# Entry to the seven-product jobs: order of the sums of x, the root and the first gates, and the engine of each chunk's last y rest

## The chip, the cores and the metric

The kernel runs on one core of a Trainium2 chip. The metric is the device time of one execution in microseconds (us). The kernel before takes 1664.19 us, the median of three runs (1663.05 to 1666.98).

## The reference, cut to what matters

Two transformer blocks in float32 over 512 tokens of width 1024. The change lies in the last part of the first block, the gated feed-forward:

```python
def rmsnorm(x, g):
    xf = x.astype(jnp.float32)
    y = xf * lax.rsqrt(jnp.mean(xf * xf, axis=-1, keepdims=True) + EPS)
    return (y * g.astype(jnp.float32)).astype(x.dtype)

def swiglu(u, w_gate_up, w_down):
    gate, up = jnp.split(u @ w_gate_up, 2, axis=-1)
    return (jax.nn.silu(gate) * up) @ w_down
...
        h = h + memory_cross_attention(...)
        h = h + swiglu(rmsnorm(h, ffn_norm[l]), w_gate_up[l], w_down[l])
    return rmsnorm(h, final_norm)
```

w_gate_up is 1024 x 5632 (D_FF = 2816, 22 tiles of 128), w_down 2816 x 1024.

## The kernel before, in words

**Products in three parts.** Activations lie transposed: features on the partitions, 512 tokens along the free axis. Every float32 product is made of three matmuls on rounded parts: hi = the value rounded to fp32r, lo = the rest; hi x hi, hi x lo and lo x hi are added in a PSUM bank. So every weight and every activation has to be *rounded* (hi) and have its *rest* (lo) taken by some engine before PE can use it. Work is cut into *jobs*, one block of 256 weight columns each. The four PSUM tiles g_bank hold job results, the four banks t_bank everything else, sums of weights and of x among them. Raw weights come by SP's DMAs into two slots w_raw, a job's slot being free when w_split has counted the split of the job two before it.

**Norm.** x_hi and x_lo hold h times the norm's gain, without the division by the root mean square; each product is multiplied by rstd afterwards. ScalarE squares h, VectorE adds the squares (add_squares, L2939), PE sums them over the partitions (squares_sum, task stat3, L1126), ScalarE takes the square root (root, L1872, with an ACT_TABLE_LOAD of its own ahead), and VectorE the reciprocal (L3002).

**Feed-forward.** The 22 tiles are three chunks (FF_CHUNKS = 8, 8, 6). A tile's job (gu) has 128 gate and 128 up columns. The first three tiles (gu0, gu0+1, gu0+2) are plain: 48 matmuls of 512 columns, after which VectorE multiplies the gate by rstd (plain_gate, L3022), ScalarE takes the silu (L2196), VectorE multiplies by up (gated_up, L3029, tile ga; it frees the job's g_bank pair), ScalarE rounds ga to y_hi (y_round), and GpSimd takes y_lo (y_rest, L915). Job gu0+2 uses the g_bank pair of gu0, so PE can start it only when gated_up(0) is done.

The other 19 tiles are made as 2 x 2 blocks with seven products in place of eight (seven_products, L1420). This takes sums of x, computed once, and sums of weights, computed for each tile. The sums of x: ScalarE copies x times gain in full precision to x32a and x32b (eight instructions of 128 x 512), VectorE makes four differences of 128 x 1024 in PSUM (x_sum, L3010; number i into banks 0 and 1 for even i, 2 and 3 for odd i), ScalarE rounds each (x_sum_hi), VectorE takes each rest (x_sum_rest, L3016). Sum i+2 overwrites the banks of sum i, so it waits for rest i. The root's operand lies in one of t_bank's banks 2 and 3. For each tile, ScalarE copies one quarter of the weights (a22_copy), VectorE makes three sums (first_sum, other_sums, L3034 to L3041), ScalarE rounds seven operands, VectorE takes three rests (sum_rest, L3047), GpSimd one difference (difference_of_weights, L893) and four rests (first_rests, last_rest, L899). A tile's fourth block waits for the gate bank of the tile before it (for the first tile: gated_up(2)).

**Chunk end.** A chunk's four down jobs follow its tiles. The first (L1483) goes through y tile by tile and waits for each y_lo (ff_lo); its weights are rounded by ScalarE into e_hi, and GpSimd takes the rest e_lo (subtract_hi, L879). The second's weights are split wholly by GpSimd (plain_split, L885 and L879) into w_hi and w_lo. In the last chunk the third and fourth are rounded by ScalarE (L2279) and their rests taken by GpSimd (L954).

**What orders the work.** Each engine's instructions stand in the order in which its block is written; semaphores alone join them. In the order before, the entry on ScalarE is: root, copies to x32, x_sum_hi(0) and (1), silu(0), x_sum_hi(2) and (3), y_round(0), silu(1), y_round(1). On VectorE: reciprocal, x_sum(0), x_sum(1), rest(0), x_sum(2), gate(0), rest(1), x_sum(3), rest(2), gated_up(0), rest(3), gate(1), gated_up(1). On GpSimd: the split of gu0+2's weights, y_rest(0), y_rest(1), then the first tile. At a chunk's end GpSimd has e_lo, the last y_rest, then the second down job's split:

```python
                pool.wait_ge(slot_hi, down_hi_count(c))
                pool.nop().then_inc(pool_chain, 1)
                subtract_hi(down, e_lo[:], e_hi[:], n)
                y_rest(c, FF_F0[c] + n - 1)
                pool.wait_ge(block_done, BLOCK0 + 6 * s + 4)
                plain_split(down + 1, w_lo[:, 0], w_hi[:, 0])
```

Of the kernel before, what the change touches and what calls it, by code (L numbers as in the profile page):

```python
# [20 lines left out]
ALU = mybir.AluOpType  # L21
ACT = mybir.ActivationFunctionType
AX = mybir.AxisListType
F32 = mybir.dt.float32
# [58 lines left out]
FF_F0 = [0, 8, 16]  # L83
# [148 lines left out]
def program(nc, A, out):  # L232
    with ExitStack() as ctx:
# [544 lines left out]
        def _(pool):  # L778
# [122 lines left out]
            def first_rests(c, j, s):  # L901

                slot_rest(c, s, 0, w_part_raw(j, 0, 0)).then_inc(slot_lo, 1)
                slot_rest(c, s, 1, w_part_raw(j, 1, 0)).then_inc(slot_lo, 1)
                slot_rest(c, s, 4, s3_raw[:]).then_inc(slot_lo, 1)
# [5 lines left out]
            def y_rest(c, tile):  # L911

                pool.wait_ge(ff_hi, tile + 1)
                k = tile - FF_F0[c]
                nc.gpsimd.tensor_tensor(y_lo[:, k, :], ga[:, tile % 2, :], y_hi[:, k, :].bitcast(F32), ALU.subtract).then_inc(ff_lo, 1)  # L915
# [4 lines left out]
            for c, n in enumerate(FF_CHUNKS):  # L920
                tiles = ff_tiles(c)
                down = JOBS[f"down{c}"]
                j, tile, s = tiles[0]
                if c == 0:
                    y_rest(c, 0)
                    y_rest(c, 1)
                difference_of_weights(j, s)
                first_rests(c, j, s)
                for i, (j, tile, s) in enumerate(tiles):
                    more = i + 1 < len(tiles)  # L930
                    if more:
                        difference_of_weights(j + 1, s + 1)
                    last_rest(c, j, s)
                    if tile > FF_F0[c]:
                        y_rest(c, tile - 1)
                    if more:
                        first_rests(c, j + 1, s + 1)
                pool.wait_ge(slot_hi, down_hi_count(c))
                pool.nop().then_inc(pool_chain, 1)
                subtract_hi(down, e_lo[:], e_hi[:], n)  # L940
                y_rest(c, FF_F0[c] + n - 1)
                pool.wait_ge(block_done, BLOCK0 + 6 * s + 4)
                plain_split(down + 1, w_lo[:, 0], w_hi[:, 0])
                if c < 2:
                    pool.wait_ge(w_used, down)
                    plain_split(down + 2, w_lo[:, 1], w_hi[:, 1])
                    pool.wait_ge(w_used, down + 1)
                    plain_split(down + 3, e_lo[:], e_hi[:])
# [903 lines left out]
        def _(act):  # L1852
            def copy(o, i, scale=1.0):
                return nc.scalar.activation(o, i, ACT.Copy, scale=scale)  # L1854
# [15 lines left out]
            def root(i, e=0):  # L1870
                b = ready(i)
                ins = nc.scalar.activation(rstd[:], b, ACT.Sqrt, bias=eps[:, e:e + 1], scale=1.0 / D)  # L1872
                link(ins)
                act.nop().then_inc(t_free[BANK[i]], 1)
                act.nop().then_inc(std_ready, 1)
# [297 lines left out]
            for i in range(4):  # L2173
# [4 lines left out]
                    copy(x_hi[:, k, :], hT[:, k, :], col["ffn_norm"](k)).then_inc(nhi_ready, 1)  # L2178
                for k in (2 * i, 2 * i + 1):
                    square(2, k)  # L2180
            root(TASKS["stat3"])

            act.wait_ge(w_used, JOBS["gu0"])
            for k in range(DT):
                ins = copy(x32[k // HK][:, k % HK, :], hT[:, k, :], col["ffn_norm"](k))
            ins.then_inc(slot_hi, 1)

            def x_sum_hi(i):

                act.wait_ge(sum_ready, 16 + max(i + 1, 2))  # L2190
                copy(xt_hi[i][:], sum_banks(i % 2)).then_inc(slot_hi, 1)

            def silu(tile, bank_):

# [20 lines left out]
                act.wait_ge(slot_lo_v, LO_V0 + 3 * s)  # L2215
                copy(sum_bank(2), w_part_raw(j, 1, 1)).then_inc(a22_ready, 1)

            x_sum_hi(0)
            x_sum_hi(1)
            silu(0, 0)  # L2220
            x_sum_hi(2)
            x_sum_hi(3)
            y_round(0, 0)
            silu(1, 2)
            y_round(0, 1)
            for c, n in enumerate(FF_CHUNKS):
# [392 lines left out]
        def _(dve):  # L2619
# [378 lines left out]
                done(v.tensor_tensor(y_lo[:, i, :], b, y_hi[:, i, :].bitcast(F32), ALU.subtract), o_lo, t_free[BANK[r]])  # L2998

            residual_and_lo(JOBS["wo1"], 2, col["ffn_norm"], x_hi, x_lo)  # L3000
            dve.wait_ge(std_ready, 2)
            link(v.reciprocal(rstd[:], rstd[:]))  # L3002
            for b in range(4):
                dve.wait_ge(t_free[b], FF_BEFORE[b])

            def x_sum(i, out, in0, in1):

# [16 lines left out]
            def gated_up(j, tile, up):  # L3024

                dve.wait_ge(sg_ready, tile + 1)
                if tile >= 2:
                    dve.wait_ge(ff_lo, tile - 1)
                done(v.tensor_tensor(ga[:, tile % 2, :], sg[:, tile % 2, :], up, ALU.mult), ga_ready, g_free[j % 2])  # L3029

            def first_sum(j, s):

# [21 lines left out]
            def add_down(c, i):  # L3054
# [10 lines left out]
                if c == 2:  # L3065
                    add_squares(3, i)

            dve.wait_ge(slot_hi, 1)
            x_sum(0, sum_banks(0), x32_part(0, 1), x32_part(0, 0))
            x_sum(1, sum_banks(1), x32_part(1, 1), sum_banks(0))  # L3070
            x_sum_rest(0)
            x_sum(2, sum_banks(0), x32_part(1, 1), x32_part(0, 1))
            plain_gate(0)
            x_sum_rest(1)
            x_sum(3, sum_banks(1), x32_part(1, 0), sum_banks(1))
            x_sum_rest(2)
            gated_up(JOBS["gu0"], 0, g_bank[:, 1, :])
            x_sum_rest(3)
            plain_gate(1)
            gated_up(JOBS["gu0"] + 1, 1, g_bank[:, 3, :])  # L3080
            for c, n in enumerate(FF_CHUNKS):
# [14 lines left out]
                for i, (j, tile, s) in enumerate(tiles):  # L3096
# [21 lines left out]
                    up_halves = g_bank[:, up, :].rearrange("p (a b) -> p a b", b=HT)  # L3118
                    link(v.tensor_tensor(up_halves, up_halves, m_sum[:, V, :].unsqueeze(1).to_broadcast([P, 2, HT]), ALU.add))
                    gated_up(j, tile, g_bank[:, up, :])  # L3120
                add_down(c, 0)
                add_down(c, 1)
            add_down(2, 2)
# [412 lines left out]
```

## Time and profile before

| | before |
|---|---|
| median of 3 runs | 1664.19 us (1663.05 to 1666.98) |
| profiled execution, own time | 1664.38 us |
| its span | 1662.7 us |
| mean granted TensorE clock | 0.997 of full |
| busy: PE, DVE, ACT, POOL | 98%, 63%, 40%, 63% |
| this stage, from the first plain job to the last down job | about 512.5 to 869.6 us |

The profile is of one execution. Its own time is the span plus what lies around it. Engines are PE (TensorE), DVE (VectorE), ACT (ScalarE), POOL (GpSimd) and SP (the queue that issues DMAs). In a timeline row the brackets give the engine's idle time just before the row and what ended it. Matmuls overlap in the pipeline, so a matmul's duration is longer than the distance between two starts. L1420 is line 1420 of the kernel; a helper's line stands for all its callers.

### The profile page before, as it was taken

To read this page: it belongs to the slowest core of one execution; us is meant where nothing else is said; L and a number is where in the kernel's file an instruction comes from. 1 tells how busy PE (TensorE), PEld (TensorE's weight loads), DVE (VectorE), ACT (ScalarE), POOL (GpSimd) and SP (SyncE) were. 2 spreads that over 40 slices of the span, in tenths; PEclk is the share of its full clock that TensorE was granted. 3 is DMA by queue.
4 is the path that set the end of the run, shared out by engine and by line. 5 is a ranking of instruction groups with operands and counts; after the bars stand their busy time and mean duration, and the time that the engine had idled before them with its cause. 6 is when DMAs were issued, how large, how long until landed. Compare 5 with 4: busy or idle time off the path is not lost.

```text
span 1662.7 us, 23770 instructions
## 1 busy us (share of the span) xinstructions
PE 1630.6 (98%) x8755; PEld 1384.0 (83%) x8755; DVE 1041.3 (63%) x1631; ACT 664.2 (40%) x1166; POOL 1040.3 (63%) x791
## 2 busy tenths in 40 slices
PE   7999999999998999999999999999999999999998
PEld 5898897888977998998978888887878778877887
DVE  5323948772446645745747898999646686556624
ACT  5431238330424523523525545674312245555301
POOL 7675764566656675775766788785467644334664
PEclk9999999999999999999999999999999999999999
DMA  6333333233243233433334333222243222111231
GB/s 210 122 108 112 118 102 121 83 101 102 83 145 101 67 112 90 111 105 93 98 105 111 101 102 95 79 81 77 76 152 97 89 76 76 53 51 52 76 114 64
DMA packets 188347, 162.59 MB, mean 98 GB/s; under 512 B 7636, under 2 KB 184400, under 8 KB 187728
## 3 DMA queue, kind: packets, MB, share of 16 engines
q1 hardware_dynamic: 188040, 161.10, 30.5%
q8 instruction: 67, 1.10, 0.3%
q14 instruction: 40, 0.33, 0.1%
q10 hardware_dynamic: 200, 0.06, 0.0%
HBM read 155.87 MB, written 4.23 MB: 96 GB/s over the span
## 4 chain that ended last, share of the span: by engine, by line
PE 90%; DVE 5%; ACT 2%; POOL 1%; issue 1%; DMA 1%; DVEq 0%; SPq 0%; ACTq 0%; POOLq 0%
PE g_bank L1046 53%; PE g_bank L1420 9%; PE g_bank L1080 6%; PE g_bank L1070 5%; PE t_bank L1759 2%; PE t_bank L1420 2%; PE g_bank L1483 1%; PE g_bank L1629 1%; PE t_bank L1771 1%; PE t_bank L1371 1%; PE t_bank L1403 1%; PE t_bank L1748 1%; PE t_bank L1547 1%; PE t_bank L1568 1%; PE g_bank L1220 1%
## 5 line engine op out<-in xcount | busy, mean ns | idle before, releaser
L803 POOL TENSOR_SCALAR w_hi<-w_raw 128x2048 fp32r<-128x2048 f32 x67 | 132.5, 1978 | 387.3 <-PE g_bank L1046 160.8
L820 POOL TENSOR_TENSOR w_lo<-w_raw,w_hi 128x512 fp32r<-128x512 f32 x264 | 367.0, 1421 | 5.5
L1046 PE MATMUL g_bank<-x_hi,w_hi 128*128 128x512 f32 x912 | 364.5, 400 | 0.4 <-DVEq L2633 0.4
L1046 PE MATMUL g_bank<-x_hi,w_lo 128*128 128x512 f32 x912 | 355.5, 390 | 0.0
L1046 PE MATMUL g_bank<-x_lo,w_hi 128*128 128x512 f32 x912 | 355.2, 390 | 0.0
L1046 PEld LDWEIGHTS g_bank<-x_hi,w_hi 128*128 128x128 f32 x912 | 171.3, 188 | 38.8 <-issue 4.8
L1046 PEld LDWEIGHTS g_bank<-x_hi,w_lo 128*128 128x128 f32 x912 | 171.2, 188 | 36.1
L1046 PEld LDWEIGHTS g_bank<-x_lo,w_hi 128*128 128x128 f32 x912 | 171.5, 188 | 35.1 <-issue 1.4
L3165 DVE SCALAR_TENSOR_TENSOR t_bank<-hc,cols,t_bank 128x512 f32<-128x512 f32 x280 | 187.0, 749 | 4.5 <-DVE hc L3149 2.7
L954 POOL TENSOR_TENSOR w_lo<-w_raw,w_hi 128x512 fp32r<-128x512 f32 x100 | 127.4, 1309 | 62.7 <-ACT w_hi L2279 62.7
L1046 PE MATMUL g_bank<-y_hi,w_hi 128*128 128x512 f32 x288 | 113.6, 394 | 2.4 <-POOL w_lo L879 2.4
L1046 PE MATMUL g_bank<-y_hi,w_lo 128*128 128x512 f32 x288 | 112.2, 390 | 0.0
L1046 PE MATMUL g_bank<-y_lo,w_hi 128*128 128x512 f32 x288 | 112.1, 389 | 0.0
L899 POOL TENSOR_TENSOR w_lo<-w_raw,w_hi 128x512 fp32r<-128x512 f32 x57 | 73.0, 1296 | 34.0 <-ACT w_hi L1854 34.0
L972 POOL TENSOR_TENSOR pacc<-pacc,prod 128x512 f32<-128x512 f32 x54 | 68.1, 1293 | 0.0
L1046 PEld LDWEIGHTS g_bank<-y_hi,w_hi 128*128 128x128 f32 x288 | 54.1, 188 | 14.9 <-POOL w_lo L879 2.8
L1420 PE MATMUL g_bank<-x_hi,w_lo 128*128 128x256 f32 x228 | 64.5, 283 | 0.0
L1420 PE MATMUL g_bank<-xt_hi,w_hi 128*128 128x256 f32 x228 | 64.5, 283 | 0.0
L1420 PE MATMUL g_bank<-xt_lo,w_hi 128*128 128x256 f32 x228 | 64.5, 283 | 0.0
L1420 PE MATMUL g_bank<-xt_hi,w_lo 128*128 128x256 f32 x228 | 64.5, 283 | 0.0
L1420 PE MATMUL g_bank<-x_lo,w_hi 128*128 128x256 f32 x228 | 64.5, 283 | 0.0
L1420 PE MATMUL g_bank<-x_hi,w_hi 128*128 128x256 f32 x228 | 64.5, 283 | 0.0
(564 smaller groups left out, 3985.3 us busy)
## 6 DMA issues: line engine op xcount, KB each, us to landing
w_raw<-w_gate_up SPq DMA_DIRECT2D x44, 512.0 KB, 4.7
w_raw<-a_w_in SPq DMA_DIRECT2D x44, 512.0 KB, 4.5
w_raw<-b_w_in SPq DMA_DIRECT2D x38, 512.0 KB, 4.4
w_raw<-w_in SPq DMA_DIRECT2D x28, 512.0 KB, 4.5
w_raw<-w_kv SPq DMA_DIRECT2D x16, 512.0 KB, 3.9
w_raw<-w_out_mix SPq DMA_DIRECT2D x16, 512.0 KB, 6.4
w_raw<-w_down SPq DMA_DIRECT2D x16, 512.0 KB, 4.1
w_raw<-a_w_out SPq DMA_DIRECT2D x16, 512.0 KB, 4.4
```

The costliest lines, as they stand in the source:

```text
L803: nc.gpsimd.tensor_scalar(w_hi[:, par], w_raw[:, par], 1.0, 0.0, ALU.mult, ALU.add).then_inc(pool_chain, 1)
L820: last = nc.gpsimd.tensor_tensor(w_lo[:, par, s], w_raw[:, par, s], w_hi[:, par, s].bitcast(F32), ALU.subtract)
L899: return nc.gpsimd.tensor_tensor(lo, src, hi.bitcast(F32), ALU.subtract)
L954: last = nc.gpsimd.tensor_tensor(lo[:, s], w_raw[:, j % 2, s], hi[:, s].bitcast(F32), ALU.subtract)
L972: nc.gpsimd.tensor_tensor(acc_k[:], acc_k[:], p[:], ALU.add).then_inc(tap_chain, 1)
L1046: last = nc.tensor.matmul(g_bank[:, 2 * pair + f if banks is None else banks[f], 0:n], ww[:, k0 + k, ws], xk, start=(k == 0 and q == 0), s ...
L1070: last = nc.tensor.matmul(g_bank[:, 2 * par + f, :], ww[:, par, k, ws], xx[:, k0 + k, :], start=(k == 0 and q == 0), stop=(k == kt - 1 and ...
L1080: last = nc.tensor.matmul(g_bank[:, 2 * par + m // 2, m % 2 * WC:m % 2 * WC + n], xx[:, k, m * P:(m + 1) * P], ww[:, k, 0:n], start=(k == ...
L1220: last = nc.tensor.matmul(g_bank[:, 2 * (j % 2) + f, :], ww[:, k, ws], xx[:, k, :], start=(k == 0 and q == 0), stop=(k == KT - 1 and q == 2))
L1420: last = nc.tensor.matmul(out, ww[:, k, :], xx[:, k, :], start=(k == 0 and q == 0), stop=(k == HK - 1 and q == 2))
L1759: last = nc.tensor.matmul(b[:, c:c + W_OF[qb]], qB[:, 4 * hg + i, qb * P:(qb + 1) * P], kB[:, 0:W_OF[qb]], start=True, stop=True)
L3165: ins = v.scalar_tensor_tensor(tail if k == TAPS - 1 else a(k), h(k), wk, a(k), ALU.mult, ALU.add)
```

## The change

Three edits. (1) ScalarE makes the copies to x32 and rounds the first sum of x ahead of the root, and VectorE makes that sum and its rest ahead of the reciprocal; only the banks that a sum writes are waited for (0 and 1, later 2 and 3). (2) The first gate product, silu and gated_up(0) stand ahead of sums 2 and 3, and y_round(0) ahead of rounding sum 2; GpSimd's y_rest(1) goes behind the first tile's first rests. (3) The last y rest of each chunk is taken by VectorE (last_y_rest) and no longer by GpSimd. PE's and SP's programs stay as they are.

```diff
--- before.py
+++ after.py
@@ -923,9 +923,10 @@
                 j, tile, s = tiles[0]
                 if c == 0:
                     y_rest(c, 0)
-                    y_rest(c, 1)
                 difference_of_weights(j, s)
                 first_rests(c, j, s)
+                if c == 0:
+                    y_rest(c, 1)
                 for i, (j, tile, s) in enumerate(tiles):
                     more = i + 1 < len(tiles)
                     if more:
@@ -938,7 +939,6 @@
                 pool.wait_ge(slot_hi, down_hi_count(c))
                 pool.nop().then_inc(pool_chain, 1)
                 subtract_hi(down, e_lo[:], e_hi[:], n)
-                y_rest(c, FF_F0[c] + n - 1)
                 pool.wait_ge(block_done, BLOCK0 + 6 * s + 4)
                 plain_split(down + 1, w_lo[:, 0], w_hi[:, 0])
                 if c < 2:
@@ -2178,17 +2178,18 @@
                     copy(x_hi[:, k, :], hT[:, k, :], col["ffn_norm"](k)).then_inc(nhi_ready, 1)
                 for k in (2 * i, 2 * i + 1):
                     square(2, k)
-            root(TASKS["stat3"])
+
+            def x_sum_hi(i):
+
+                act.wait_ge(sum_ready, 16 + i + 1)
+                copy(xt_hi[i][:], sum_banks(i % 2)).then_inc(slot_hi, 1)
 
             act.wait_ge(w_used, JOBS["gu0"])
             for k in range(DT):
                 ins = copy(x32[k // HK][:, k % HK, :], hT[:, k, :], col["ffn_norm"](k))
             ins.then_inc(slot_hi, 1)
-
-            def x_sum_hi(i):
-
-                act.wait_ge(sum_ready, 16 + max(i + 1, 2))
-                copy(xt_hi[i][:], sum_banks(i % 2)).then_inc(slot_hi, 1)
+            x_sum_hi(0)
+            root(TASKS["stat3"])
 
             def silu(tile, bank_):
 
@@ -2215,12 +2216,11 @@
                 act.wait_ge(slot_lo_v, LO_V0 + 3 * s)
                 copy(sum_bank(2), w_part_raw(j, 1, 1)).then_inc(a22_ready, 1)
 
-            x_sum_hi(0)
+            silu(0, 0)
             x_sum_hi(1)
-            silu(0, 0)
+            y_round(0, 0)
             x_sum_hi(2)
             x_sum_hi(3)
-            y_round(0, 0)
             silu(1, 2)
             y_round(0, 1)
             for c, n in enumerate(FF_CHUNKS):
@@ -2998,10 +2998,6 @@
                 done(v.tensor_tensor(y_lo[:, i, :], b, y_hi[:, i, :].bitcast(F32), ALU.subtract), o_lo, t_free[BANK[r]])
 
             residual_and_lo(JOBS["wo1"], 2, col["ffn_norm"], x_hi, x_lo)
-            dve.wait_ge(std_ready, 2)
-            link(v.reciprocal(rstd[:], rstd[:]))
-            for b in range(4):
-                dve.wait_ge(t_free[b], FF_BEFORE[b])
 
             def x_sum(i, out, in0, in1):
 
@@ -3027,6 +3023,13 @@
                 if tile >= 2:
                     dve.wait_ge(ff_lo, tile - 1)
                 done(v.tensor_tensor(ga[:, tile % 2, :], sg[:, tile % 2, :], up, ALU.mult), ga_ready, g_free[j % 2])
+
+            def last_y_rest(c, tile):
+
+                k = tile - FF_F0[c]
+                dve.wait_ge(ff_hi, tile + 1)
+                dve.wait_ge(ff_lo, tile)
+                v.tensor_tensor(y_lo[:, k, :], ga[:, tile % 2, :], y_hi[:, k, :].bitcast(F32), ALU.subtract).then_inc(ff_lo, 1)
 
             def first_sum(j, s):
 
@@ -3065,16 +3068,22 @@
                 if c == 2:
                     add_squares(3, i)
 
+            for b in range(2):
+                dve.wait_ge(t_free[b], FF_BEFORE[b])
             dve.wait_ge(slot_hi, 1)
             x_sum(0, sum_banks(0), x32_part(0, 1), x32_part(0, 0))
+            x_sum_rest(0)
+            dve.wait_ge(std_ready, 2)
+            link(v.reciprocal(rstd[:], rstd[:]))
+            plain_gate(0)
+            for b in range(2, 4):
+                dve.wait_ge(t_free[b], FF_BEFORE[b])
             x_sum(1, sum_banks(1), x32_part(1, 1), sum_banks(0))
-            x_sum_rest(0)
+            gated_up(JOBS["gu0"], 0, g_bank[:, 1, :])
             x_sum(2, sum_banks(0), x32_part(1, 1), x32_part(0, 1))
-            plain_gate(0)
             x_sum_rest(1)
             x_sum(3, sum_banks(1), x32_part(1, 0), sum_banks(1))
             x_sum_rest(2)
-            gated_up(JOBS["gu0"], 0, g_bank[:, 1, :])
             x_sum_rest(3)
             plain_gate(1)
             gated_up(JOBS["gu0"] + 1, 1, g_bank[:, 3, :])
@@ -3118,6 +3127,7 @@
                     up_halves = g_bank[:, up, :].rearrange("p (a b) -> p a b", b=HT)
                     link(v.tensor_tensor(up_halves, up_halves, m_sum[:, V, :].unsqueeze(1).to_broadcast([P, 2, HT]), ALU.add))
                     gated_up(j, tile, g_bank[:, up, :])
+                last_y_rest(c, tile)
                 add_down(c, 0)
                 add_down(c, 1)
             add_down(2, 2)
```

VectorE at the entry, from the end of the sums of squares to the second gated product; before (xt_lo_134 to xt_lo_137 are the rests of the sums of x 0 to 3):

```order
L3002 RECIPROCAL rstd<-rstd 128x512
L3010 TENSOR_TENSOR t_bank<-x32a 128x1024
L3010 TENSOR_TENSOR t_bank<-x32b,t_bank 128x1024
L3016 TENSOR_TENSOR xt_lo_134<-t_bank,xt_hi_130 128x1024
L3010 TENSOR_TENSOR t_bank<-x32b,x32a 128x1024
L3022 TENSOR_TENSOR g_bank<-g_bank,rstd 128x512
L3016 TENSOR_TENSOR xt_lo_135<-t_bank,xt_hi_131 128x1024
L3010 TENSOR_TENSOR t_bank<-x32b,t_bank 128x1024
L3016 TENSOR_TENSOR xt_lo_136<-t_bank,xt_hi_132 128x1024
L3029 TENSOR_TENSOR ga<-sg,g_bank 128x512
```

The same place in the changed kernel:

```order
L3006 TENSOR_TENSOR t_bank<-x32a 128x1024
L3012 TENSOR_TENSOR xt_lo_134<-t_bank,xt_hi_130 128x1024
L3077 RECIPROCAL rstd<-rstd 128x512
L3018 TENSOR_TENSOR g_bank<-g_bank,rstd 128x512
L3006 TENSOR_TENSOR t_bank<-x32b,t_bank 128x1024
L3025 TENSOR_TENSOR ga<-sg,g_bank 128x512
L3006 TENSOR_TENSOR t_bank<-x32b,x32a 128x1024
L3012 TENSOR_TENSOR xt_lo_135<-t_bank,xt_hi_131 128x1024
L3006 TENSOR_TENSOR t_bank<-x32b,t_bank 128x1024
L3012 TENSOR_TENSOR xt_lo_136<-t_bank,xt_hi_132 128x1024
L3012 TENSOR_TENSOR xt_lo_137<-t_bank,xt_hi_133 128x1024
L3018 TENSOR_TENSOR g_bank<-g_bank,rstd 128x512
```

Sum 0 and its rest went ahead of the reciprocal. Between reciprocal and first ga there were eight instructions, now there are two.

ScalarE at the entry, as one piece of the difference:

```order
 L1854 ACTIVATE x_hi<-hT,cols 128x512 x2
 L2111 ACTIVATE nring<-hT 128x512 x2
-L1872 ACT_TABLE_LOAD
-L1872 ACTIVATE rstd<-t_bank,eps 128x512
 L1854 ACTIVATE x32a<-hT,cols 128x512 x4
 L1854 ACTIVATE x32b<-hT,cols 128x512 x4
 L1854 ACTIVATE xt_hi_130<-t_bank 128x1024
+L1872 ACT_TABLE_LOAD
+L1872 ACTIVATE rstd<-t_bank,eps 128x512
+L2197 ACT_TABLE_LOAD
+L2197 ACTIVATE sg<-g_bank 128x512
 L1854 ACTIVATE xt_hi_131<-t_bank 128x1024
```

The root with its table load went behind the eight copies and the rounding of sum 0.

GpSimd at the end of chunk 2 (the same piece stands at the ends of chunks 0 and 1, with x4 for e_lo):

```order
 L915 TENSOR_TENSOR y_lo<-ga,y_hi 128x512
 L879 TENSOR_TENSOR e_lo<-w_raw,e_hi 128x512 x3
-L915 TENSOR_TENSOR y_lo<-ga,y_hi 128x512
 L885 TENSOR_SCALAR w_hi<-w_raw 128x2048
 L879 TENSOR_TENSOR w_lo<-w_raw,w_hi 128x512 x4
```

The split of the second down job's weights now stands right behind e_lo.

## Rows read from the trace of the kernel before

**Rows 1.** the page, busy time of the engines
```profile
PE 1630.6 (98%) x8755; PEld 1384.0 (83%) x8755; DVE 1041.3 (63%) x1631; ACT 664.2 (40%) x1166; POOL 1040.3 (63%) x791
```

**Rows 2.** timeline of PE at the entry: start us, us, engine, line, operation, tiles
```profile
534.89 0.39 PE L1046 MATMUL g_bank<-x_hi,w_lo 128*128 128x512 f32 x1
541.86 0.77 PE L1046 MATMUL g_bank<-x_hi,e_hi 128*128 128x512 f32 x1 [6.58 <-DVEq L2633]
...
555.25 0.28 PE L1420 MATMUL g_bank<-x_hi,w_hi 128*128 128x256 f32 x1
```

**Rows 3.** granted clock and busy times, 542 to 549 us: window; length; busy us (instructions)
```profile
542.00:549.00 7.00, 7.00 (x21) 5.55 (x22) 4.40 (x6) 3.65 (x8) 4.50 (x4) 0.65 0.01 2
```

**Rows 4.** chain of waits, entry: start us, us, what
```profile
512.61 10.88 PE g_bank L1070 x48
```

**Rows 5.** waits of PE, 560 to 870 us: us in total, times, longest us
```profile
PE g_bank L1046 <- POOL w_lo L879: 2.4, 1, 2.4
```

**Rows 6.** timeline of ACT at the entry
```profile
515.89 1.28 ACT L1872 ACT_TABLE_LOAD   x1
524.39 0.69 ACT L1872 ACTIVATE rstd<-t_bank,eps 128x512 f32<-128x512 f32 x1 [7.21 <-PE t_bank L1126]
525.28 2.56 ACT L1854 ACTIVATE x32a<-hT,cols 128x512 f32<-128x512 f32 x4 [0.20 <-ACT rstd L1872]
...
532.95 1.94 ACT L1854 ACTIVATE xt_hi<-t_bank 128x1024 fp32r<-128x1024 f32 x2 [2.66 <-DVE t_bank L3010]
```

**Rows 7.** timeline of DVE at the entry
```profile
516.88 3.48 DVE L2939 TENSOR_TENSOR sq_sum<-sq_sum,nring 128x512 f32<-128x512 f32 x2
525.31 3.35 DVE L3002 RECIPROCAL rstd<-rstd 128x512 f32<-128x512 f32 x1 [4.95 <-ACTq L1875]
530.42 1.23 DVE L3010 TENSOR_TENSOR t_bank<-x32a 128x1024 f32<-128x1024 f32 x1 [1.76 <-ACT x32b L1854]
...
540.88 0.68 DVE L3029 TENSOR_TENSOR ga<-sg,g_bank 128x512 f32<-128x512 f32 x1
...
544.29 0.69 DVE L3029 TENSOR_TENSOR ga<-sg,g_bank 128x512 f32<-128x512 f32 x1 [0.66 <-ACT sg L2196]
...
550.54 0.69 DVE L3047 TENSOR_TENSOR w_lo<-t_bank,w_hi 128x512 fp32r<-128x512 f32 x1 [0.21 <-ACT w_hi L1854]
```

**Rows 8.** all instructions of line 2939: durations in ns, min/median/max
```profile
L2939 DVE TENSOR_TENSOR sq_sum<-sq_sum,nring x21: 678/1666/1778, 352.0 to 873.2; 128x512 f32<-128x512 f32 x21
```

**Rows 9.** timeline of ACT, a table load elsewhere
```profile
874.73 1.28 ACT L2289 ACT_TABLE_LOAD   x1
876.03 0.20 ACT L2289 ACTIVATE ltok<-eps 128x1 f32<-128x1 f32 x1
```

**Rows 10.** timeline of POOL at the entry
```profile
521.48 1.91 POOL L885 TENSOR_SCALAR e_hi<-w_raw 128x2048 fp32r<-128x2048 f32 x1
523.48 5.04 POOL L879 TENSOR_TENSOR e_lo<-w_raw,e_hi 128x512 fp32r<-128x512 f32 x4
```

**Rows 11.** timeline of PE after chunk 2's first down job
```profile
844.64 0.50 PE L1046 MATMUL g_bank<-y_hi,w_hi 128*128 128x512 f32 x1 [2.38 <-POOL w_lo L879]
```

**Rows 12.** timeline of POOL around the end of chunk 2
```profile
828.22 3.80 POOL L879 TENSOR_TENSOR e_lo<-w_raw,e_hi 128x512 fp32r<-128x512 f32 x3 [0.17 <-ACT e_hi L1854]
836.33 1.28 POOL L915 TENSOR_TENSOR y_lo<-ga,y_hi 128x512 fp32r<-128x512 f32 x1 [4.32 <-ACT y_hi L1854]
...
839.59 5.00 POOL L879 TENSOR_TENSOR w_lo<-w_raw,w_hi 128x512 fp32r<-128x512 f32 x4
844.54 5.47 POOL L954 TENSOR_TENSOR w_lo<-w_raw,w_hi 128x512 fp32r<-128x512 f32 x4
```

**Rows 13.** w_raw, 824 to 842 us: DMA issues, time to landing
```profile
L604 SPq DMA_DIRECT2D w_raw<-w_down x4: 367/428/489, 826.6 to 832.5; - x4
...
DMA to landing us min/median/max: 3.0/3.5/3.8
```

**Rows 14.** timeline of ACT after chunk 2's first down job
```profile
842.29 1.91 ACT L2279 ACTIVATE w_hi<-w_raw 128x2048 fp32r<-128x2048 f32 x1 [6.04 <-PE g_bank L1483]
```

## The prediction

> **What bounds the kernel now.** The page comes first: TensorE (PE) is busy for 98% of the span, the other compute engines for 40 to 63% [rows 1]. So time can come only from what PE waits for and from the clock at which it works; a faster VectorE (DVE), ScalarE (ACT) or GpSimd (POOL) is worth nothing by itself. I looked for PE's gaps where the change is. The timeline shows one at the entry: the last matmul of job gu0+1 begins at 534.89, the first of gu0+2 at 541.86, after 6.58 us of idling that ended with a semaphore from VectorE [rows 2]. The matmul behind the gap takes 0.77 instead of 0.39, and from 542 to 549 the granted clock is 0.65 of full, so PE sat partly at the lower level, 1.2 GHz, after that idle stretch [rows 3]. A job of 48 matmuls at full clock takes 10.88 [rows 4]; gu0+2 takes 13.39, from 541.86 to the first matmul of the seven-product tile at 555.25 [rows 2]. The whole rest of the stage, 560 to 870, holds one more wait, 2.4 us for a split by GpSimd [rows 5].
>
> **The entry, before.** ScalarE has loaded the square root's table by 517.2 and then idles 7.21 until the root at 524.39; only behind it come the eight copies of x [rows 6]. VectorE idles 4.95, takes the reciprocal at 525.31 (3.35), waits for the copies and starts the first sum at 530.42. The first gate product ends at 541.56 (540.88 + 0.68), and PE starts 0.30 later [rows 7, 2].
>
> **The entry, after, step by step.** The copies need 5.14 (525.28 until the sum that they release at 530.42). They can start where the table load stands now, 515.89, so they release VectorE at 521.03; its sums of squares end at 520.36 (516.88 + 3.48) [rows 6, 7].
> x_sum(0) takes 1.23 with GpSimd idle. It reads two tiles in SBUF, and now GpSimd is splitting weights beside it. That is not in the trace of before for this operation; the nearest row is the sum of squares, which also reads two SBUF tiles: 0.68 at least, 1.78 at most [rows 8]. I take the difference, 1.1, since that row was taken beside the same work: 2.33, to 523.36. Bounds: 0, and 1.9 for waiting out GpSimd's whole rounding of 1.91 [rows 10].
> The Trainium skill, page "SBUF — State Buffer", section Who interferes with whom, says that such a DVE instruction and a GpSimd one that reads SBUF exclude each other for a whole instruction; by it the upper bound would be the value. The entry sum would end near 524.6 and PE would be served about 0.8 later than worked out here.
> Then x_sum_hi(0) 1.0 (two took 1.94), the table load 1.28, no longer hidden, and the root 0.69 [rows 6]: 526.35. PE has the root's operand ready at 524.36, so the root moves 2 us later; this is the price of putting the sum ahead. Reciprocal 0.23 behind the root and 3.35 long: 529.95. Gate product 0.69, x_sum(1) 1.24 with the silu (0.66) beside it, ga 0.68, release 0.30 [rows 7]: PE may start at **532.9**. It is free at 534.89 + 0.23 = 535.12, so 2.2 us are spare, 1.4 at the upper bound, 3.3 at the lower. GpSimd's split of the weights of gu0+2 ends at 528.5 (523.48 + 5.04) [rows 10], with 1.9 of delay at 530.4: also in time. The gap goes whole: 541.86 - 535.12 = **6.74**.
> Without the gap nothing asks the clock to fall: gu0+2 takes 10.88 and not 13.39: **2.51**. Its end is then 546.0.
> A page states more for the table load. The trace has 1.28 for it, and elsewhere an activation starts 0.02 after such a load ended [rows 9]. "ScalarE: Activation LUTs", section What ACT_TABLE_LOAD costs, in the Trainium skill, adds a drain of some 1.38 to each switch; by it the gate would still come in time, and the next step would be late (rival 1).
>
> **What is late next.** The three sums and four rests left over now stand between the first and the second gate. From the end of ga(0), 532.6: five operations of 1.24, gate product, silu: ga(1) starts at 540.15 (in the old order 3.4 after ga(0), now 7.5). From the start of ga(1) to the end of the last rest of the first tile's sums it was 550.54 + 0.69 - 544.29 = 6.94 [rows 7]: 547.1. Gate(2), silu and ga(2) add 0.69 + 0.66 + 0.69, and 0.30: 549.45. The fourth block of the first tile waits for that; it is due at 546.0 plus three blocks of 12 half-width matmuls, 1.36 each, 550.1. Spare: 0.6 us; at the upper bound of the first sum a wait of 0.2, at the lower 1.7 spare. Should x_sum(2) also meet a GpSimd operation (1.1), 0.5 to 1.3 are lost. I take 0. GpSimd's own first rests, 1.28 each [rows 12], come before the second y rest now, and are due at 546.0 and 547.4; started near 543 they end at 544.3 and 545.6. The moved y rest and the next difference have till 556.1.
>
> **The chunk ends.** In chunk 2 PE ends the first down job and waits 2.38 for w_lo of the second [rows 11]. GpSimd had finished e_lo at 832.02, idled 4.32 for the last y_hi, made y_lo (1.28), and only then split the second job's weights, 836.33 + 1.28 to 844.59, 6.98 long [rows 12]. With the y rest on VectorE the split starts at 832.02 and ends at 839.0, for a PE that is free at 842.10. The load is no new wait: issued from 826.6 in two parts, at most 3.8 to land, so there by about 831 [rows 13]. The rest on VectorE reads two SBUF tiles, 0.68 to 1.78 by rows 8, from about 836.35; its engine is idle there, and PE needs y_lo for the sixth step near 840.7. It may hold GpSimd's split up by 0.7, into 3 us of spare. Gain: 844.64 - 842.10 = **2.54**. Next late is the third job: ScalarE rounds from 842.29 for 1.91 [rows 14], GpSimd takes 5.47 [rows 12], so 849.7; PE comes at 842.10 + 8.16 (36 matmuls) = 850.3. Spare 0.6. In chunks 0 and 1 PE has no wait at this place [rows 5], so the same edit is worth nothing there.
>
> **The sum.** 6.74 + 2.51 + 2.54 = 11.8 off the profiled execution's 1664.38: 1652.6. Against the median of the runs, 1664.19, it is **1652.4**. The profiled execution stands 0.2 above that median.
>
> **Rivals.** 0.2% of the time, 3.3 us, is about what a measurement here can tell from no change.
> 1. *The fourth block waits.* For: 0.6 of spare is less than one contended operation. Against: no such wait at 557, and the steps are priced from rows. With 1.2 lost, 1653.6. An idle of some 1.4 behind the new table load, which rows 9 speak against, would end in the same place: 0.8 lost, 1653.2, and I give it 0.02 of this rival's chance. That is the drain that the Trainium skill's page "ScalarE: Activation LUTs" names in the section cited above.
> 2. *The chunk end does not pay*: GpSimd is held up, or the third job's weights take the same 2.5. For: 0.6 spare there too. 1654.9.
> 3. *GpSimd holds the first sum until its whole split is done*, 528.5. The sum then ends at 529.75, 6.4 later: PE starts gu0+2 at 539.3, with 4.2 of the gap left and perhaps the slow clock (0 to 2.5). The gain at the entry is 2.5 to 5.0; about 1658.5. Against: in rows 8 no operation lost more than 1.1.
> 4. *The change does not do what it says*, since the gate still comes at 541.6 for a cause that I don't see; with the chunk end, 1661.7, no change that can be told.
> 5. *Slower.* Engines enter the 19 seven-product tiles with less in hand, and GpSimd, last in line for each tile, holds PE up in all of them instead of once. Its price is the lag per tile: over 11.8 / 19 = 0.62 us in each the change loses, and at 0.9 it would give 1664.2 - 11.8 + 17.1 = 1669.5. For: GpSimd starts the first tile 4 us later relative to PE than before. Against: six operations of 1.28 are 7.7 us in a tile of at least 7 x 1.36 = 9.5, so a lag shrinks by about 2 us in each.
>
> **How the numbers follow.** Forecast 0.73; rival 1 0.12, rival 2 0.06, rival 3 0.04, rival 4 0.03, rival 5 0.02. Cases 1 to 3 and the forecast are faster by more than 3.3: 0.95; rival 4 is the same: 0.03; rival 5 slower: 0.02. The range reaches below by 1.9, since both medians may be off by about the 1.1 that the lowest run of before lies under its own, and above to rivals 1 and 2 together, 1652.4 + 1.2 + 2.5 = 1656.1. It is 1650.5 to 1656.1.
>
> **What would show it.** Right: no PE wait between 534 and 556, clock 1.00 in the stretch of gu0+2, L1872 at about 525.7, reciprocal near 526.6, first ga end near 532.6, no wait for the split in front of chunk 2's second down job. Wrong in part: a PE wait ahead of the fourth block of the first tile, or one in front of the third down job. Wrong as a whole: x_sum(0) longer than 3.1 us, or short waits in many L1420 blocks.

## The result and the profile after

The changed kernel takes 1652.34 us, the median of four runs (1651.63 to 1652.55); the kernel before took 1663.89 beside it (four runs, 1663.05 to 1666.98). The ratio is 0.9926, with a 95% interval of 0.9914 to 0.9938. The prediction was 1652.4, with a range of 1650.5 to 1656.1.

The profiled execution of the changed kernel took 1652.55 us, its span is 1650.8, 11.9 less than before. The page, its busy times and the order of the engines in them, as [rows 1]:

```profile
PE 1627.0 (99%) x8755; PEld 1381.9 (84%) x8755; DVE 1046.3 (63%) x1634; ACT 664.6 (40%) x1166; POOL 1039.3 (63%) x788
```

PE at the three places of [rows 2], the last matmul of gu0+1, the first of gu0+2, the first of the seven-product tiles:

```profile
534.86 0.39 PE L1046 MATMUL g_bank<-x_hi,w_lo 128*128 128x512 f32 x1
535.08 0.39 PE L1046 MATMUL g_bank<-x_hi,e_hi 128*128 128x512 f32 x1
...
545.96 0.28 PE L1420 MATMUL g_bank<-x_hi,w_hi 128*128 128x256 f32 x1
```

No idle time stands in a bracket, the first matmul of gu0+2 has its 0.39, and the job takes 545.96 - 535.08 = 10.88. The clock in the windows that held the gap and the slow matmuls (window, length, then busy us and instructions of PE, PEld, DVE, ACT, POOL, then the granted clock, DMA share and GB/s), as [rows 3]:

```profile
535.00:542.00 7.00, 7.00 (x33) 5.79 (x32) 5.05 (x6) 3.46 (x6) 0.68 (x2) 1.00 0.00 0
542.00:549.00 7.00, 7.00 (x45) 6.30 (x44) 5.16 (x9) 4.97 (x11) 6.27 (x6) 1.00 0.00 0
```

The waits of PE from 505 to 860, asked as in [rows 5], are none. The chain of waits through the entry, start and length in us, is now PE alone, where VectorE and ScalarE stood in it before:

```profile
512.58 10.88 PE g_bank L1070 x48
523.46 0.86 PE t_bank L1126 x2
524.32 21.81 PE g_bank L1046 x96
546.13 2.87 PE g_bank L1420 x24
```

VectorE at the entry, as [rows 7] (the sum of x is at line 3006, its rest at 3012, the reciprocal at 3077, the gate at 3018, ga at 3025, the first tile's rests at 3050):

```profile
516.86 3.48 DVE L2939 TENSOR_TENSOR sq_sum<-sq_sum,nring 128x512 f32<-128x512 f32 x2
520.88 1.69 DVE L3006 TENSOR_TENSOR t_bank<-x32a 128x1024 f32<-128x1024 f32 x1 [0.54 <-ACT x32b L1854]
523.74 1.22 DVE L3012 TENSOR_TENSOR xt_lo<-t_bank,xt_hi 128x1024 fp32r<-128x1024 f32 x1 [1.16 <-ACT xt_hi L1854]
525.79 3.35 DVE L3077 RECIPROCAL rstd<-rstd 128x512 f32<-128x512 f32 x1 [0.83 <-ACTq L1875]
529.18 0.70 DVE L3018 TENSOR_TENSOR g_bank<-g_bank,rstd 128x512 f32<-128x512 f32 x1
529.79 1.22 DVE L3006 TENSOR_TENSOR t_bank<-x32b,t_bank 128x1024 f32<-128x1024 f32 x1
531.04 0.69 DVE L3025 TENSOR_TENSOR ga<-sg,g_bank 128x512 f32<-128x512 f32 x1
...
539.39 0.69 DVE L3025 TENSOR_TENSOR ga<-sg,g_bank 128x512 f32<-128x512 f32 x1 [0.67 <-ACT sg L2197]
...
545.64 0.69 DVE L3050 TENSOR_TENSOR w_lo<-t_bank,w_hi 128x512 fp32r<-128x512 f32 x1 [0.20 <-ACT w_hi L1854]
...
547.60 0.69 DVE L3025 TENSOR_TENSOR ga<-sg,g_bank 128x512 f32<-128x512 f32 x1 [0.66 <-ACT sg L2197]
```

ScalarE, as [rows 6]:

```profile
515.74 2.56 ACT L1854 ACTIVATE x32a<-hT,cols 128x512 f32<-128x512 f32 x4
...
522.61 1.03 ACT L1854 ACTIVATE xt_hi<-t_bank 128x1024 fp32r<-128x1024 f32 x1 [1.86 <-DVE t_bank L3006]
523.65 1.28 ACT L1872 ACT_TABLE_LOAD   x1
524.95 0.69 ACT L1872 ACTIVATE rstd<-t_bank,eps 128x512 f32<-128x512 f32 x1
525.82 1.28 ACT L2197 ACT_TABLE_LOAD   x1 [0.18 <-ACT rstd L1872]
```

GpSimd, as [rows 10]:

```profile
521.46 2.88 POOL L885 TENSOR_SCALAR e_hi<-w_raw 128x2048 fp32r<-128x2048 f32 x1
524.42 5.02 POOL L879 TENSOR_TENSOR e_lo<-w_raw,e_hi 128x512 fp32r<-128x512 f32 x4
532.73 1.62 POOL L915 TENSOR_TENSOR y_lo<-ga,y_hi 128x512 fp32r<-128x512 f32 x1 [3.28 <-ACT y_hi L1854]
```

The end of chunk 2, GpSimd and then VectorE, as [rows 12]:

```profile
818.86 3.80 POOL L879 TENSOR_TENSOR e_lo<-w_raw,e_hi 128x512 fp32r<-128x512 f32 x3 [0.18 <-ACT e_hi L1854]
822.63 1.91 POOL L885 TENSOR_SCALAR w_hi<-w_raw 128x2048 fp32r<-128x2048 f32 x1
824.63 5.51 POOL L879 TENSOR_TENSOR w_lo<-w_raw,w_hi 128x512 fp32r<-128x512 f32 x4
834.94 5.49 POOL L954 TENSOR_TENSOR w_lo<-w_raw,w_hi 128x512 fp32r<-128x512 f32 x4 [4.81 <-ACT w_hi L2279]
```

```profile
826.93 0.80 DVE L3032 TENSOR_TENSOR y_lo<-ga,y_hi 128x512 fp32r<-128x512 f32 x1 [0.76 <-ACT y_hi L1854]
```

**Where the time came from.** The profile was cut by starts on PE. All columns are distances in us: from the sum of squares (L1126) to the first matmul of gu0+2; from there to the first seven-product matmul; from there to chunk 0's first down job; in chunk 2 from the first down job to the second; from that to the first memory job. The last is the whole stage from the sum of squares to the memory job, with the parts between that are not shown (they sum to 228.20 to 228.27 in every row). The first rows are the two kernels; the others are the experiments below.

| kernel | to gu0+2 | gu0+2 | tiles of chunk 0 | down job, chunk 2 | to memory job | stage |
|---|---|---|---|---|---|---|
| before | 18.53 | 13.39 | 50.39 | 10.73 | 24.79 | 346.10 |
| after | 11.78 | 10.88 | 50.40 | 8.18 | 24.67 | 334.11 |
| e1_entry_only | 11.78 | 10.88 | 50.40 | 10.72 | 24.82 | 336.86 |
| e2_rest_only | 18.52 | 12.88 | 50.39 | 8.19 | 24.64 | 342.82 |
| e3_rest_last_chunk | 11.79 | 10.88 | 50.39 | 8.18 | 24.66 | 334.10 |
| e4_gates_late | 13.67 | 11.00 | 50.39 | 8.19 | 24.68 | 336.13 |
| e5_root_first | 11.79 | 11.54 | 51.32 | 8.18 | 24.64 | 335.67 |
| e6_delay1 | 11.79 | 10.88 | 50.39 | 8.19 | 24.66 | 334.11 |
| e6_delay3 | 11.79 | 11.27 | 51.34 | 8.18 | 24.69 | 335.47 |
| e6_delay6 | 15.50 | 12.58 | 50.40 | 8.18 | 24.69 | 339.55 |
| e7_second_y_rest_first | 11.79 | 10.88 | 50.39 | 8.18 | 24.65 | 334.09 |
| e8_y_rest_first_and_delay3 | 11.79 | 12.67 | 50.46 | 8.19 | 24.64 | 335.95 |

The stage lost 11.99: 6.75 of the gap, 2.51 of the slow clock behind it, 2.55 in chunk 2, 0.12 in front of the memory job, and the rest in the parts not shown. The whole time of one execution moves by about 1 us from one to the next for a cause outside the stage (PE's first wait, for a DMA of parameters, lasted from 9.1 to 10.6 us in these profiles), so the stage tells tenths apart where the medians don't.

### The profile page after: what moved, and what is told of

It is laid out like the page before. It is cut to its first block, busy times and chain, and to the rows that moved or that the text cites. A ratio compares the mean times of both kernels' runs of the same rounds, so it can differ in the third digit from the quotient of the medians.

```text
span 1650.8 us, 23774 instructions
## 1 busy us (share of the span) xinstructions
PE 1627.0 (99%) x8755; PEld 1381.9 (84%) x8755; DVE 1046.3 (63%) x1634; ACT 664.6 (40%) x1166; POOL 1039.3 (63%) x788
## 4 chain that ended last, share of the span: by engine, by line
PE 93%; DVE 4%; ACT 1%; DMA 1%; issue 1%; POOL 0%; DVEq 0%; SPq 0%; ACTq 0%
PE g_bank L1046 54%; PE g_bank L1420 10%; PE g_bank L1080 6%; PE g_bank L1070 5%; PE g_bank L1483 2%; PE t_bank L1420 2%; PE t_bank L1759 2%; PE g_bank L1629 1%; PE t_bank L1771 1%; PE t_bank L1371 1%; PE t_bank L1403 1%; PE t_bank L1748 1%; PE t_bank L1547 1%; PE t_bank L1568 1%; PE g_bank L1611 1%; PE t_bank L1304 1%
## 5 line engine op out<-in xcount | busy, mean ns | idle before, releaser
L1046 PEld LDWEIGHTS g_bank<-y_hi,w_hi 128*128 128x128 f32 x288 | 54.1, 188 | 11.9 <-issue 0.7
```

Source lines behind the costliest of these rows:

```text
L1046: last = nc.tensor.matmul(g_bank[:, 2 * pair + f if banks is None else banks[f], 0:n], ww[:, k0 + k, ws], xk, start=(k == 0 and q == 0), s ...
```

## The experiments

The theory: the gain is PE's two waits and the clock lost behind the longer one, and nothing else; the entry is worth 9.3, the chunk-end edit 2.5, in chunk 2 alone. Rivals: the relief of GpSimd at all chunk ends carries much of it; the early sum, or the early gate, alone carries the entry; VectorE's chain is the bound at the entry, so that each of its delays costs.

**The entry alone: e1_entry_only.**

```diff
 subtract_hi(down, e_lo[:], e_hi[:], n)
+y_rest(c, FF_F0[c] + n - 1)
...
-last_y_rest(c, tile)
```

> The changed kernel with each chunk's last y rest back on GpSimd. Theory: the entry carries 9.3 us (6.7 of gap, 2.5 of slow clock) and the chunk ends 2.5, so this takes about 1654.9 and PE waits 2.4 us for w_lo in front of chunk 2's second down job, and nowhere else between 505 and 860. Rival (GpSimd, relieved at three chunk ends, carries a good part of the gain): well above 1656.

Measured: 1655.51 us, ratio to the kernel before 0.9951 (0.9938 to 0.9965). Its only wait of PE between 505 and 862 (us in total, times, longest):

```profile
PE g_bank L1047 <- POOL w_lo L879: 2.4, 1, 2.4
```

GpSimd in the same kernel has the old order, with 4.32 of idling for the last y_hi ahead of the y rest:

```profile
818.76 3.80 POOL L879 TENSOR_TENSOR e_lo<-w_raw,e_hi 128x512 fp32r<-128x512 f32 x3 [0.17 <-ACT e_hi L1855]
826.88 1.28 POOL L915 TENSOR_TENSOR y_lo<-ga,y_hi 128x512 fp32r<-128x512 f32 x1 [4.32 <-ACT y_hi L1855]
828.13 1.92 POOL L885 TENSOR_SCALAR w_hi<-w_raw 128x2048 fp32r<-128x2048 f32 x1
830.13 4.99 POOL L879 TENSOR_TENSOR w_lo<-w_raw,w_hi 128x512 fp32r<-128x512 f32 x4
```

The stage is 2.75 longer than in the changed kernel, 2.54 of it at this wait. The rival asked for well over 1656, and falls: outside the wait the relief of GpSimd is worth 0.2.

**The chunk ends alone: e2_rest_only.**

```diff
 subtract_hi(down, e_lo[:], e_hi[:], n)
-y_rest(c, FF_F0[c] + n - 1)
...
+last_y_rest(c, tile)
 add_down(c, 0)
```

> The kernel before with only the last y rests moved to VectorE. Theory: 2.5 us under the kernel before, about 1661.5; the 6.6 us wait at the entry and the slow clock behind it stay as they were. Rival: 5 us or more are gained, since GpSimd is free 4 us earlier at three places.

Measured: 1661.39 us, ratio 0.9982 (0.9973 to 0.9991). The down job in chunk 2 went from 10.73 to 8.19, as with the whole change. The wait at the entry is there with its 6.6:

```profile
PE g_bank L1045 <- DVEq L2632: 6.6, 1, 6.6
```

The stage is 3.28 shorter than before, 0.7 more than the wait. Of that, 0.51 is gu0+2 at 12.88 in place of 13.39: behind the same 6.58 of idling PE worked for a shorter time at the low clock (the last section has the rows). So the price of the slow clock differed by half a microsecond between these two executions, for a cause that is not in the edit.

**Chunk 2 only: e3_rest_last_chunk.**

```diff
 subtract_hi(down, e_lo[:], e_hi[:], n)
+if c < 2:
+    y_rest(c, FF_F0[c] + n - 1)
...
-last_y_rest(c, tile)
+if c == 2:
+    last_y_rest(c, tile)
```

> The changed kernel with the last y rest on VectorE in chunk 2 only, on GpSimd in chunks 0 and 1. Theory: the same time as the changed kernel, 1652.3, no wait of PE between 505 and 860. Rival (GpSimd's earlier release at the first two chunk ends is worth something too): slower than the changed kernel by up to 2.5 us a chunk.

Measured: 1651.65 us, ratio 0.9921 (0.9908 to 0.9935), and a stage of 334.10 against 334.11. The moved rests of chunks 0 and 1 are worth nothing, though GpSimd is free 4 us earlier there too: PE never waited for it at these places. It was close: in this kernel the old order ends chunk 0's split at 607.22 (602.20 + 5.02) and PE starts the second down job at 607.41; in chunk 1 it is 731.39 for 731.60. What sets chunk 2 apart is its six tiles in place of eight. The old order ends the split 10.7 behind the start of the first down job in both (607.22 - 596.51 here, 844.59 - 833.91 in chunk 2 of the kernel before), but with 36 matmuls and not 48 that job takes 8.19 there and not 10.90.

**The early sum without the early gate: e4_gates_late.**

```diff
 # ScalarE
-silu(0, 0)
 x_sum_hi(1)
-y_round(0, 0)
+silu(0, 0)
 x_sum_hi(2)
 x_sum_hi(3)
+y_round(0, 0)
 # VectorE
-plain_gate(0)
 x_sum(1, ...)
-gated_up(JOBS["gu0"], 0, ...)
 x_sum(2, ...)
+plain_gate(0)
 x_sum_rest(1)
 x_sum(3, ...)
 x_sum_rest(2)
+gated_up(JOBS["gu0"], 0, ...)
 x_sum_rest(3)
```

> The changed kernel with the first gate, silu and ga back behind sums 1, 2 and 3; sum 0 stays ahead of the root. Theory: behind the reciprocal (ending at 529.1) stand six operations of 1.2 and the gate's 0.6 before ga: ga ends at 536.8, PE is served at 537.1 and wants to start at 535.1, so a wait of 2.0; about 1654.3 if TensorE's clock stays full, up to 1656.8 if it falls as it did behind the 6.6 us wait. Rival (the sums ahead of the root are what closes the gap, the place of the gate does not count): 1652.3, no wait.

Measured: 1653.66 us, ratio 0.9939 (0.9926 to 0.9953), with one wait:

```profile
PE g_bank L1046 <- DVEq L2633: 1.7, 1, 1.7
```

gu0+2 starts 1.9 later than in the changed kernel, for a forecast of 2.0, so the rival (the place of the gate does not count) falls. The job takes 11.00: the granted clock stayed at 1.00 behind 1.73 of idling. So the early sum alone gives back some 4.9 of the 6.75 of the gap and nearly all of the slow clock; the early gate is worth the last 2.0.

**The early gate without the early sum: e5_root_first.** Some waits go back to those of the kernel before and are not shown here: x_sum_hi(0) waits for two sums again, and VectorE for all four banks at once.

```diff
 # ScalarE
+root(TASKS["stat3"])
 act.wait_ge(w_used, JOBS["gu0"])
 for k in range(DT):
     ins = copy(x32[...], ...)
 ins.then_inc(slot_hi, 1)
-x_sum_hi(0)
-root(TASKS["stat3"])
 silu(0, 0)
+x_sum_hi(0)
 x_sum_hi(1)
 # VectorE
+dve.wait_ge(std_ready, 2)
+link(v.reciprocal(rstd[:], rstd[:]))
+plain_gate(0)
 x_sum(0, ...)
-x_sum_rest(0)
-dve.wait_ge(std_ready, 2)
-link(v.reciprocal(rstd[:], rstd[:]))
-plain_gate(0)
 x_sum(1, ...)
 gated_up(JOBS["gu0"], 0, ...)
+x_sum_rest(0)
 x_sum(2, ...)
```

> The changed kernel with the root ahead of the copies and of sum 0 again, and the reciprocal and the first gate ahead of all sums. Theory: ga(0) ends near 533.6 and is in time for PE at 535.1, so the gap stays closed; but all eight sums and rests stand behind the reciprocal, ga(1) starts near 542.6 instead of 539.4, and PE waits about 1.5 us at the fourth block of the first seven-product tile: 1653.8. Rival (the early sum is needed to close the gap): a wait of several us in front of job gu0+2, 1656 or more.

Measured: 1653.87 us, ratio 0.994 (0.9926 to 0.9953). The gap in front of gu0+2 is closed, by the gate alone; the rival falls. Two short waits come in its place:

```profile
PE g_bank L1420 <- DVEq L2633: 0.6, 1, 0.6
PE g_bank L1420 <- POOL w_lo L899: 0.5, 1, 0.5
```

(A listed wait is shorter than the time lost between starts, since the matmul ahead counts as busy to its modelled end and the first one behind is longer: 0.39 and not 0.28 at the fourth block.) The sum of the losses was right (1.56 by the stage, 1.5 expected), their place only in part. 0.9 fell on the fourth block, as named; 0.66 on the first block, where PE waited for GpSimd's rest of the first slot, which I had counted as in time. All of VectorE's eight sums and rests stand between the first gate and ga(1) here (in the changed kernel two of them stand ahead of the reciprocal), and ga(1) sets when ScalarE rounds that slot, since y_round(1) is ahead of it in ScalarE's queue:

```profile
528.83 0.70 DVE L3018 TENSOR_TENSOR g_bank<-g_bank,rstd 128x512 f32<-128x512 f32 x1
530.56 1.23 DVE L3006 TENSOR_TENSOR t_bank<-x32a 128x1024 f32<-128x1024 f32 x1 [1.03 <-ACT x32b L1854]
...
542.82 0.69 DVE L3025 TENSOR_TENSOR ga<-sg,g_bank 128x512 f32<-128x512 f32 x1 [0.67 <-ACT sg L2196]
```

So each of the two moves closes most or all of the gap alone. Together they are 1.6 to 2.0 us better than either, and each is limited by another wait.

**How much is spare: e6_delay1, e6_delay3, e6_delay6.** Rest 0 of the sums of x is done again, to the same place, one, three or six times.

```diff
 x_sum_rest(0)
+dve.wait_ge(slot_lo_v, 17)
+for _ in range(1):          # 3 in e6_delay3, 6 in e6_delay6
+    link(v.tensor_tensor(xt_lo[0][:], sum_banks(0), xt_hi[0][:].bitcast(F32), ALU.subtract))
 dve.wait_ge(std_ready, 2)
```

> The changed kernel with rest 0 of the sums of x done once more on VectorE ahead of its wait for the root: 1.3 us more, of which 0.8 fall into its idle time there, so gate and sums come 0.5 later. Theory: spare are 3.0 us at the start of gu0+2 and 1.7 at the fourth block, so nothing is lost: 1652.3, no wait. Rival (VectorE's chain is the bound of the entry): 0.5 us slower.

One execution, 1653.09 us; no wait of PE, and a stage of 334.11, the same as without the delay. VectorE's chain is not the bound.

> Rest 0 three times more. Theory: the chain is 3.2 us later: 0.2 lost at the start of gu0+2 and 1.3 at the fourth block of the first tile, together the delay less the spare 1.7: 1653.8. Rival: 3.2 lost, 1655.5.

One execution, 1653.56 us. The stage is 1.36 longer. The reciprocal starts at 528.35, against 525.79 in the changed kernel; all of PE's events up to there lie 0.45 earlier in this profile (gu0 begins at 511.97 and not at 512.42), so the chain is 3.0 later, and 3.0 less the spare 1.7 is 1.3. But the loss again has two places:

```profile
PE g_bank L1420 <- DVEq L2633: 0.6, 1, 0.6
PE g_bank L1420 <- POOL w_lo L899: 0.2, 1, 0.2
```

0.39 at the first block and 0.94 until the fourth. At the start of gu0+2 nothing was lost, where 0.2 was expected.

> Rest 0 six times more. Theory: the chain is 7.3 us later: PE waits 4.2 in front of gu0+2. If TensorE's clock stays full behind it, another 1.4 is lost at the fourth block, 1657.9; if it falls as behind the 6.6 us wait of the kernel before, 4.2 and up to 2.5 are lost and the fourth block does not wait, 1659.0.

One execution, 1658.09 us, the stage 5.44 longer: 3.7 in front of gu0+2 and 1.7 in gu0+2 itself, which took 12.58; no wait at the fourth block. The delay was 6.8 and not 7.3 (six repeats took 7.52), and 6.8 less the spare of 3.05 is 3.7. So the clock did fall, and for a while only: it was at the lower level from 539.60 to 543.01, and half of these 3.41 us is the 1.7. PE behind the wait:

```profile
538.68 0.47 PE L1046 MATMUL g_bank<-x_hi,e_hi 128*128 128x512 f32 x1 [3.55 <-DVEq L2633]
538.98 0.39 PE L1046 MATMUL g_bank<-x_lo,e_hi 128*128 128x512 f32 x1
...
539.45 0.50 PE L1046 MATMUL g_bank<-x_hi,e_hi 128*128 128x512 f32 x1
539.75 0.63 PE L1046 MATMUL g_bank<-x_lo,e_hi 128*128 128x512 f32 x1
...
542.31 0.63 PE L1046 MATMUL g_bank<-x_lo,e_hi 128*128 128x512 f32 x1
...
543.10 0.40 PE L1046 MATMUL g_bank<-x_hi,e_hi 128*128 128x512 f32 x1
543.33 0.39 PE L1046 MATMUL g_bank<-x_lo,e_hi 128*128 128x512 f32 x1
```

**The second y rest: e7_second_y_rest_first and, with the delay, e8_y_rest_first_and_delay3.**

```diff
 y_rest(c, 0)
+y_rest(c, 1)
 difference_of_weights(j, s)
 first_rests(c, j, s)
-if c == 0:
-    y_rest(c, 1)
```

> The changed kernel with GpSimd's second y rest back in front of the first tile's difference and rests. Theory: GpSimd's rest for the first block then ends near 544.7 (y rest 1.3 and difference 1.3 behind the second y_hi at 540.8) for a PE that comes at 546.0: no wait, the stage from the sum of squares to the first memory job as long as in the changed kernel, 334.1. Rival (this third part carries some of the gain): PE waits at the first block.

One execution, 1652.56 us, stage 334.09: this part of the change is worth nothing by itself. What the old place does is push GpSimd's first rest from 541.92 to 542.99, by 1.46, since PE's events lie 0.39 earlier in this profile; the spare time there is 2.6.

> The same edit together with rest 0 done three times more on VectorE. With the delay alone PE lost 0.4 at the first block (GpSimd) and 1.0 at the fourth (VectorE), 1.4 in all. Theory: y rest and difference push GpSimd's first rest to about 547.9, so PE loses 2.0 at the first block and nothing at the fourth: stage 336.1. Rival (GpSimd's order does not matter): 335.5, as with the delay alone.

One execution, 1653.7 us, stage 335.95: 0.5 more than the same delay with the new order of GpSimd. 1.79 was lost at the first block, where 2.0 was expected, and 0.06 until the down job. PE's one wait is at the first block (timeline; the bracket has the idle time and what ended it):

```profile
547.01 0.36 PE L1419 MATMUL g_bank<-x_hi,w_hi 128*128 128x256 f32 x1 [1.59 <-POOL w_lo L899]
```

So the order of GpSimd matters only when the chain ahead of it is late; in the changed kernel it isn't.

## Why the prediction was right, step by step

- **What bounds.** PE's waits were the right thing to count. The gap went whole: 18.53 - 11.78 = 6.75 against 6.74; the clock 2.51 against 2.51; chunk 2's down job 2.55 against 2.54. e1, e2 and e3 show that these parts stand apart and add up: 9.3 at the entry, 2.5 in chunk 2, nothing in chunks 0 and 1. That the sum is right to a tenth is in part luck: the term for the clock was read off one execution, and from that of e2_rest_only, with the same gap, it would have been 2.00.
- **The first sum beside GpSimd.** Priced 2.33, it took 1.69 (bounds 1.23 to 3.1). GpSimd paid too: its rounding of 128 x 2048, 1.91 in [rows 10], took 2.88. In e5, where the same sum runs at 530.56 with GpSimd idle, it takes 1.23, and in that kernel GpSimd's rounding has its 1.91 back. The Trainium skill, page "SBUF — State Buffer", section Who interferes with whom, has an exclusive lock for such a pair. This trace fits it: the sum was issued at 520.88 with GpSimd's last quarter of a split running until 521.46, waited for that, and GpSimd's next instruction, begun at 521.46, took 0.97 more, about the 1.1 that the sum still ran. What I had wrong is which GpSimd instruction the sum would meet: the end of a quarter, not the whole rounding. The prediction's two figures for that case also don't agree: behind the whole rounding the sum would end at 521.48 + 1.91 + 1.23 = 524.6, which is 1.3 later than the 523.36 of the forecast and not 0.8; 0.8 goes with a hold of 1.9 from 521.03.
- **The root behind the sum.** Forecast for its activation 525.66, happened 524.95; for the reciprocal 526.6, 525.79; for the release of PE 532.9, about 532.0 (531.04 + 0.69 + 0.30). The spare time was 3.05 and not 2.2, inside the bounds of 1.4 to 3.3. The price of putting the sum ahead was overstated in the words: 2 us is how long the forecast root ends behind its operand; against the old place, 524.39, the root was to start 1.3 later and started 0.56 later.
- **The table load.** The root started 0.02 after its load had ended (523.65 + 1.28, then 524.95), so the load cost 1.28 and no drain behind it. The page "ScalarE: Activation LUTs", section What ACT_TABLE_LOAD costs, in the Trainium skill, adds 1.38 to that; here the trace decides against it, and the load of [rows 9] does as well.
- **What is late next.** From the start of ga(1) to the end of the last rest there were 545.64 + 0.69 - 539.39 = 6.94, the same as forecast. (The prediction speaks of three sums and four rests between the gates; three of each are left, and its five operations behind ga(0) count them rightly.) ga(2) was ready at 548.6 for a block that came at 550.28: 1.7 spare and not 0.6, by the shorter first sum (0.6), by steps on VectorE and ScalarE that lie closer together than I added them up (0.2), and because a block of 12 half-width matmuls takes 1.44 and not 1.36. e6_delay3 gives the same 1.7 (3.0 late, 1.3 lost), and e6_delay1, 0.6 late without a loss, agrees. The step that I took too lightly is GpSimd's first rest: its spare, 2.6, hangs on the same chain, and behind a late chain both e5 and e6_delay3 lose there first.
- **The chunk end.** The split began right behind e_lo, at 822.63, and ended at 830.1, for a PE that came at 832.74. The y rest took 0.80 on VectorE in chunk 2, and the split 0.5 more (5.51 in place of 5.00). The third job's weights were in time.
- **The rivals.** Rival 1 did not happen, but its place was right: with the chain 3.0 late, PE does wait at the fourth block. Rivals 2 and 4 did not happen. Rival 3 needed a hold of 6.4 by GpSimd: the first sum was held by 0.46. Rival 5: the tiles of chunk 0 took 50.40 after 50.39, and PE has no wait up to 862, so no lag was carried through the tiles.

## What to carry to other kernels

A wait of the bounding engine is worth its own length, and, behind the waits of 3.55 and 6.58 here, half of the time that PE then worked at the lower clock; so look at what the first matmuls behind a gap cost before pricing an edit. When a chain is reordered, work out the spare time at each of the next places where it is waited for, for each engine in it: here two consumers (the fourth block through VectorE, the first through GpSimd) hung on one chain with 1.7 and 2.6 us to spare. An edit that relieves an engine at several like places pays only at those where someone waited for it: one of three here, the one whose job ahead is short.

## What the runs showed of the hardware that was not expected

- Behind an idle stretch TensorE's clock need not be low at once. After 3.55 us of idling in e6_delay6 the matmuls of 538.98 and 539.21 still took 0.39 and 0.40; from 539.75 they took 0.63 (the lower level, 1.2 GHz), and from 543.10 0.40 again. After 6.58 of idling before, the first matmul was slow already (0.77). After 1.73 (e4) and 2.38 (the chunk end of the kernel before) none was.
- The same idle stretch of 6.58 was followed by a job of 13.39 in one kernel and 12.88 in another, with nothing changed at this place. The stretch at the lower clock was equally long in both, 6.83; it began 0.9 earlier in e2_rest_only, so more of it fell into the idle time. The stretches at the lower clock, in the kernel before, in e2_rest_only and in e6_delay6 (columns as in [rows 3]; the granted clock is 1.00 on both sides of each):

```profile
540.12:546.95 6.83, 5.09 (x12) 4.06 (x13) 4.64 (x6) 3.75 (x7) 2.45 (x2) 0.50 0.01 2
539.22:546.05 6.83, 4.06 (x10) 3.22 (x11) 4.96 (x6) 3.09 (x5) 1.42 (x2) 0.50 0.01 2
539.60:543.01 3.41, 3.41 (x10) 2.62 (x9) 3.31 (x4) 1.63 (x2) 2.63 (x2) 0.50 0.02 5
```

  The loss is half of PE's busy time in the stretch: 2.5, 2.0 and 1.7 by these rows, and 2.51, 2.00 and 1.70 by the length of gu0+2. PE had stopped at about 535.3, 535.4 and 535.1, and in e6_delay6 it had been at work again for 0.9 when the clock fell. What sets the moment of the fall is not shown. The low clock may cost more in some executions: three of the kernel before, 1666.39, 1666.71 and 1666.73, have a mean clock of 0.995 where the others beside them have 0.997; no trace of them is kept.
- Where a VectorE instruction with two inputs in SBUF meets one of GpSimd, the one that comes second takes longer, on either engine. The first sum of x took 0.46 more (1.69 for 1.23) behind GpSimd's quarter, and GpSimd's rounding behind that sum 0.97 more (2.88 for 1.91). Sum 2 was first at 531.97 and kept its 1.23, while the y rest on GpSimd that began at 532.73 took 1.62 for 1.28; in e5_root_first the same pair overlaps more, and the y rest takes 2.10.
